# Attention of the first layers: half of the convolution and its norm behind the scores, two groups' squares summed on 32 columns each

## The chip, the cores and the metric

The kernel runs on one core of a Trainium2 chip. A core has a matrix engine (TensorE, PE in the profile, its weight loads as PEld), VectorE (DVE), ScalarE (ACT), GpSimd (POOL) and SyncE (SP), each with a queue of its own that it works through in order. The metric is the device time of one execution in microseconds (us).

## The reference

Four transformer layers on a sequence of 256 tokens and a width of 1024 in fp32. Layers 0 and 1 have a mixer with four parts of 256 features each; each part is brought to unit root mean square over its 256 features, multiplied by a gain, and the four go through the output projection:

```
outs = jnp.stack([short_conv_mixer(a_h, a_b, a_c, conv_w),   # group 0
                  nsa_mixer(...), gla_mixer(...), gmlp_mixer(...)], axis=2)   # groups 1, 2, 3
outs = rms_norm(outs, grp_gain.reshape(4, 256))
return outs.reshape(B, S, D_MODEL) @ w_o

def short_conv_mixer(h_in, b_gate, c_gate, conv_w):
    z = c_gate * h_in
    return b_gate * causal_conv_of_width_3(z, conv_w)
```

`nsa_mixer` is attention with three branches (compressed blocks, selected blocks, window), four heads of 64, summed with three gates. Layers 2 and 3 are of another kind and are not touched.

## The kernel before, in words

Features lie on partitions where this text speaks of columns: `oT` is 128 x 8 x 256, two chunks of 256 tokens for each group; `convT` holds the three inputs of the convolution in the same form. All matrix products with weights take three products of high and low halves; ScalarE makes the high half of a weight slot (L449), VectorE the low half (L458), GpSimd both halves of the activations (L890, L892). `rows_half` (L908) multiplies half a slot of the output projection into four banks of the accumulator PS. Everything is ordered by hand: each phase appends to the queue of each engine, and semaphores (`sig(...)`) join them. There is no barrier between phases.

In the phase `proj` (`gemm_phase`, L592) of layers 0 and 1 the short mixers run beside the input projection. VectorE's last piece of work there is the whole convolution (L1396 to L1406): one product of 128x512, then for each of two chunks one scaling (L1401) and two multiply-adds (L1404), and the gate product of 128x512 (L1406).

The phase `mixed` (`nsa_out_phase`) follows on each engine:

- TensorE: eight rounds of scores (L1562) in banks 3 to 7 and the compressed scores (L1613); the first four rounds come before, the last four after the sums of squares of groups 2, 3 and 0 (L1590, twelve products with one moving column, each recorded as two instructions); then `spread_group` for groups 2 and 3 (L1596), which writes a row of 1/rms over all partitions; transposes of the probabilities (L1571) and of the compressed ones (L1576), the first slot of the output projection (L908), the spread for group 0, the compressed branch (L1649), half of slot 1, then `attend(0, 0)` and `attend(1, 2)` (L1582, branches one and two of attention, 12 products each), the transposes of the finished heads (L436), and the rest of the output projection (L908, then L957), between which lie the sum and the spread for group 1.
- VectorE: masks and row maxima of the scores (L1730, L1737), the compressed scores (L1759 to L1764), the reciprocal of six columns of roots (L1766), the other scores with `normed(0)` and `normed(1)` among them (L1744), copies out of PS (L1787, L1790), `normed(2)` for the convolution's group, in layer 0 the modulation sums (L469, eight instructions), the weights of the branches (L1808), and the three branches: br 0 is L1817, br 1 and br 2 are L1819 and L1820 each. Then the copy of the heads to `oT` (L1827).
- ScalarE: three squares (L1671), the root (L1690), the exponentials (L1679), copies (L1683), weight halves (L449).

The order of VectorE between the copies and the branches, before the change:

```
normed(2, 2, 0)
for what, n, q, kk in todo:        # modulation sums, layer 0 only
    if what == "mod":
        mod_sums(dve, order, n, q, kk)
```

and of TensorE around the two `attend`s: `attend(0, 0)`, `pe.wait_ge(*on.at(6))`, `attend(1, 2)`. The signal `on` counts the halves of `normed`, two each; `gsum`, `grt`, `grc` and `gsp` count sums, roots, reciprocals and spreads.

## Time and profile before

| | us |
|---|---|
| median of 3 runs | 1518.88 (1517.07 to 1520.52) |
| profiled execution, its own time | 1518.78 |
| span of that execution | 1517.1 |
| TensorE busy | 1437.3 (95%) |
| VectorE busy | 1084.3 (71%) |
| ScalarE busy | 762.5 (50%) |
| mean granted TensorE clock | 0.988 of full |

The span is the time from the first to the last instruction; the time of the execution is 1.7 us longer. An engine's busy time counts its own instructions; a chain of waits is followed back from the last instruction of the program. PEclk is the granted TensorE clock: 1.00 is 2.4 GHz and 0.50 is 1.2 GHz.

### The profile page before, as it was taken

To read this page: it belongs to the slowest core of one execution; us is meant where nothing else is said; L and a number is where in the kernel's file an instruction comes from. 1 tells how busy PE (TensorE), PEld (TensorE's weight loads), DVE (VectorE), ACT (ScalarE), POOL (GpSimd) and SP (SyncE) were. 2 spreads that over 40 slices of the span, in tenths; PEclk is the share of its full clock that TensorE was granted. 3 is DMA by queue.
4 is the path that set the end of the run, shared out by engine and by line. 5 is a ranking of instruction groups with operands and counts; after the bars stand their busy time and mean duration, and the time that the engine had idled before them with its cause. 6 is when DMAs were issued, how large, how long until landed. Compare 5 with 4: busy or idle time off the path is not lost.

```text
span 1517.1 us, 24648 instructions
## 1 busy us (share of the span) xinstructions
PE 1437.3 (95%) x10229; PEld 1329.3 (88%) x10229; DVE 1084.3 (71%) x1448; ACT 762.5 (50%) x1097; POOL 406.7 (27%) x391
## 2 busy tenths in 40 slices
PE   2899899999999999999998899999999999999998
PEld 2888799977899799977998888999889998799987
DVE  5887797799557697799776567776477667565544
ACT  3556465534656465434875346444364444454432
POOL 0221320398121030397000321101419421220022
PEclk9999899999999999999999999999999999999999
DMA  9783659799352469798342025777557656455650
GB/s 392 278 321 118 236 232 350 290 350 346 112 209 84 165 267 347 286 350 330 139 168 98 1 87 215 287 288 261 194 191 283 218 218 226 172 198 219 223 207 28
DMA packets 49502, 340.71 MB, mean 225 GB/s; under 512 B 6640, under 2 KB 7024, under 8 KB 9072
## 3 DMA queue, kind: packets, MB, share of 16 engines
q1 hardware_dynamic: 46224, 333.04, 58.8%
q10 hardware_dynamic: 3168, 6.10, 1.1%
q8 instruction: 81, 1.33, 0.3%
q14 instruction: 29, 0.24, 0.0%
HBM read 338.04 MB, written 1.08 MB: 224 GB/s over the span
## 4 chain that ended last, share of the span: by engine, by line
PE 74%; DVE 10%; POOL 9%; issue 3%; ACT 3%; DMA 1%; SPq 0%; POOLq 0%; DVEq 0%; ACTq 0%
PE PS L592 48%; PE PS L908 14%; POOL acts_hi_lo L890 5%; POOL acts_hi_lo L892 4%; DVE ring L469 2%; DVE weights_hi_lo L458 1%; DVE X L1033 1%; PE PS L957 1%; PE PS L564 1%; DVE spare L771 1%; DVE arena L1030 1%; PE PS L2508 1%; DVE arena L1032 1%; ACT spare L736 1%; DMA X<-in_x_dram 1%
## 5 line engine op out<-in xcount | busy, mean ns | idle before, releaser
L458 DVE TENSOR_TENSOR weights_hi_lo<-ring,weights_hi_lo 128x1024 fp32r<-128x1024 f32 x426 | 550.5, 1316 | 279.1 <-ACT weights_hi_lo L449 278.0
L449 ACT ACTIVATE weights_hi_lo<-ring 128x1024 fp32r<-128x1024 f32 x426 | 444.7, 1058 | 476.4 <-PE PS L592 272.0
L592 PE MATMUL PS<-hi,weights_hi_lo 128*128 128x256 f32 x3456 | 546.2, 282 | 9.9 <-ACT hi L730 8.3
L592 PEld LDWEIGHTS PS<-hi,weights_hi_lo 128*128 128x128 f32 x3456 | 467.7, 189 | 13.0 <-issue 11.1
L908 PE MATMUL PS<-weights_hi_lo,acts_hi_lo 128*128 128x512 f32 x1584 | 377.6, 399 | 3.6 <-DVE heads L1730 2.0
L908 PEld LDWEIGHTS PS<-weights_hi_lo,acts_hi_lo 128*128 128x128 f32 x1584 | 298.4, 189 | 77.1 <-issue 2.7
L890 POOL CAST acts_hi_lo<-arena 128x256 fp32r<-128x256 f32 x142 | 134.3, 946 | 783.4 <-PE PS L908 436.0
L592 PE MATMUL PS<-lo,weights_hi_lo 128*128 128x256 f32 x1728 | 339.3, 281 | 0.0
L592 PEld LDWEIGHTS PS<-lo,weights_hi_lo 128*128 128x128 f32 x1728 | 263.0, 189 | 0.2 <-DVE lo L777 0.2
L469 DVE CUSTOM_DVE_ANT_0 ring<-ring,cond 128x1024 f32<-128x1024 f32 x192 | 253.2, 1356 | 9.7 <-DMA ring<-in_stream_dram 8.7
L892 POOL TENSOR_TENSOR acts_hi_lo<-arena,acts_hi_lo 128x256 fp32r<-128x256 f32 x142 | 170.1, 1198 | 11.4
L592 PE MATMUL PS<-weights_hi_lo,hi 128*128 128x256 f32 x928 | 150.8, 284 | 3.7 <-DVE weights_hi_lo L458 3.5
L592 PEld LDWEIGHTS PS<-weights_hi_lo,hi 128*128 128x128 f32 x928 | 127.4, 188 | 5.7 <-issue 5.5
L592 PE MATMUL PS<-weights_hi_lo,lo 128*128 128x256 f32 x464 | 93.2, 282 | 0.0
L592 PEld LDWEIGHTS PS<-weights_hi_lo,lo 128*128 128x128 f32 x464 | 71.7, 189 | 0.0
L712 PE MATMUL PS<-turning,X 128*128 128x128 f32 x256 | 33.9, 288 | 38.3 <-DVE turning L765 38.3
L712 PEld LDWEIGHTS PS<-turning,X 128*128 128x128 f32 x256 | 31.1, 199 | 40.6 <-DVE turning L765 40.6
L957 PE MATMUL PS<-weights_hi_lo,acts_hi_lo 128*128 128x512 f32 x192 | 46.3, 396 | 1.9 <-POOL acts_hi_lo L892 1.9
L2359 POOL TENSOR_TENSOR arena<-arena,constS 128x1024 f32<-128x1024 f32 x6 | 12.4, 2069 | 125.9 <-DVE arena L2276 119.6
L957 PEld LDWEIGHTS PS<-weights_hi_lo,acts_hi_lo 128*128 128x128 f32 x192 | 35.8, 187 | 11.4 <-POOL acts_hi_lo L892 2.8
L736 ACT ACTIVATE spare<-PS,mods 128x128 f32<-128x128 f32 x68 | 26.1, 454 | 9.2 <-DVE stat L875 5.1
L720 ACT ACTIVATE arena<-X 128x512 f32<-128x512 f32 x32 | 20.0, 625 | 19.7 <-DVE X L1033 11.6
(369 smaller groups left out, 1130.7 us busy)
## 6 DMA issues: line engine op xcount, KB each, us to landing
ring<-in_stream_dram SPq DMA_DIRECT2D x313, 1024.0 KB, 4.9
gate_row<-gate_rows_dram ACTq DMA_DIRECT2D x8, 512.0 KB, 3.6
constS<-in_const_dram SPq DMA_DIRECT2D x1, 1856.0 KB, 8.9
cond<-in_rows_dram SPq DMA_DIRECT2D x2, 512.0 KB, 5.2
X<-in_x_dram ACTq DMA_DIRECT2D x1, 1024.0 KB, 9.9
smallS<-in_small_dram SPq DMA_DIRECT2D x1, 883.0 KB, 8.0
out_dram<-X SPq DMA_DIRECT2D x2, 256.0 KB, 2.0
out_dram<-X ACTq DMA_DIRECT2D x2, 256.0 KB, 2.0
```

What stands on the lines that cost most here:

```text
L449: act.activation(wsp[:, g % 2, 0, at:at + HALF], ring[:, n % RING, at:at + HALF], ACT.Copy).then_inc(*ready.one())
L458: dve.tensor_tensor(wsp[:, g % 2, 1, at:at + HALF], ring[:, n % RING, at:at + HALF], wsp[:, g % 2, 0, at:at + HALF].bitcast(F32), ALU.subt ...
L469: ins = dve.tensor_tensor_reduce(w[:, r, :], w[:, r, :], cond[:, 0 if q < 12 else 1, :], 1.0, 0.0, ALU.mult, ALU.add, mods[:, q, k:k + 1])
L564: mm = pe.matmul(PS[:, 0, m * 256:(m + 1) * 256], h[:, k, m * P:(m + 1) * P], w[:, k, :], start=m + k + j == 0, stop=k == KD - 1 and j == ...
L592: mm = pe.matmul(o, lhs, rhs, start=k + g + j == 0, stop=k == KD - 1 and j == 2, skip_group_check=True)
L712: mm = pe.matmul(turned(2 * m + k // 4, k % 4), X[:, m, k * P:(k + 1) * P], turning[:, m, :], start=True, stop=True)
L720: act.activation(junk[:, u % 2, :], quarter(X, u), ACT.Square, accum_out=sums[:, u:u + 1]).then_inc(*xsq.one())
L736: ins = act.activation(buf(u)[:, k, :], turned(u, k), ACT.Identity, bias=mods[:, q, kk:kk + 1], scale=mods[:, q + 1, kk:kk + 1])
L890: pool.tensor_copy(asp[:, a % 2, 0, g, :], src).then_inc(*acts_hi.one())
L892: pool.tensor_tensor(asp[:, a % 2, 1, g, :], src, asp[:, a % 2, 0, g, :].bitcast(F32), ALU.subtract).then_inc(*acts_lo.one())
L908: mm = pe.matmul(PS[:, banks[2 * m + half], :], x[:, g, m * P:(m + 1) * P], w[:, g, half * WIDE:(half + 1) * WIDE], start=fresh and g + j ...
L957: mm = pe.matmul(PS[:, y_banks[u], :], x[:, g, m * P:(m + 1) * P], w[:, g, side * WIDE:(side + 1) * WIDE], start=fresh and last + g + j == ...
```

## The change

`convolve` is now a function for one chunk. In `proj` VectorE does the first product and chunk 0 only. In `mixed`, at the place where `normed(2)` stood, it does chunk 1 and the gate product; the sums for group 0 are taken alone, on bank 1, after half of slot 1; the reciprocal for it follows br 0, its spread stands between the two `attend`s, and `normed(2)` follows br 1. `attend(1, 2)` stands behind the wait for that reciprocal. The sums for groups 2 and 3 are taken by four products with 256 moving columns against 32 columns of ones, group 2 into partitions 0 to 31, group 3 into 32 to 63; the root and the reciprocal then work on 64x256 values, and two products of 64 rows against a column of the identity spread them.

```
...
             def token_major(i):
                 return 0 if i < 2 or i in CONV else (140 if i == 11 else 256)
             CONV = {8: 0, 9: 4, 10: 2}
+
+            def convolve(dve, order, ch):
+
+                z, y = convT[:, 4:6, :], oT[:, 0:2, :]
+                cw = prm(f"conv{l}")
+                if ch == 0:
+                    order(dve.tensor_tensor(z, z, convT[:, 0:2, :], ALU.mult))
+                tap = [cw[:, 3 * ch + j:3 * ch + j + 1] for j in range(3)]
+                order(dve.tensor_scalar(y[:, ch, :], z[:, ch, :], tap[2], None, ALU.mult))
+                for j in (1, 0):
+                    dl = 2 - j
+                    order(dve.scalar_tensor_tensor(y[:, ch, dl:], z[:, ch, :SEQ - dl], tap[j], y[:, ch, dl:],
+                                                   ALU.mult, ALU.add))
+
+            def gate_convolved(dve):
+                y = oT[:, 0:2, :]
+                return dve.tensor_tensor(y, y, convT[:, 2:4, :], ALU.mult)
+
             def proj(blk):
                 nsa_pe, nsa_act, blocks, rotation = nsa_inputs(l, kvcT, QK, VN)
-                pe, act, dve, pool = short_mixers(l, convT, lqT, lkT, lrT, LV, LG, MU, MV, oT, blocks, rotation)
+                pe, act, dve, pool = short_mixers(l, convT, lqT, lkT, lrT, LV, LG, MU, MV, oT, blocks, rotation, convolve)
                 gemm_phase(blk, ("proj", l), token_major, evac, banks=3, split_weights=True,
                            beside=(side_by_side(pe, nsa_pe), side_by_side(act, nsa_act), dve, pool))
 
-            return proj, lambda blk: nsa_out_phase(blk, l, VN, oT), oT[:, 2:4, :]
+            return proj, lambda blk: nsa_out_phase(blk, l, VN, oT, convolve, gate_convolved), oT[:, 2:4, :]
 
         def side_by_side(*works):
 
...
 
             return pe_beside, act_beside, blocks, rotation
 
-        def short_mixers(l, convT, lqT, lkT, lrT, LV, LG, MU, MV, oT, blocks, rotation):
+        def short_mixers(l, convT, lqT, lkT, lrT, LV, LG, MU, MV, oT, blocks, rotation, convolve):
 
 
 
...
             on = area(S + 2560, TT, 256)
             gsq, g = area(5920, 8, HD), area(6432, TT, 256)
             gw = prm(f"ws{l}").rearrange("p (g t) -> p g t", g=4)
-            cw = prm(f"conv{l}")
             dq = 32 ** -0.5
             taken = sig("gemm_bank_taken")
             zp, zb, ez, lz, dd, ee, kk, tr, tk = (sig(n) for n in (
...
             d4 = d.rearrange("p (n t) -> p n t", n=4)
             V8 = MV.rearrange("p m (h d) -> p (m h) d", d=HD)
             done = sig("short_mixed")
-            state["shorts_mixed"] = {"banks": done.at(2), 2: done.at(2), 3: done.at(1), 0: done.at(3)}
+            state["shorts_mixed"] = {"banks": done.at(2), 2: done.at(2), 3: done.at(1)}
 
             def pool_beside(pool):
                 order = Order(pool, "pool_order")
...
                 yield
 
                 dve.wait_ge(*taken.at(11))
-                z, y = convT[:, 4:6, :], oT[:, 0:2, :]
-                order(dve.tensor_tensor(z, z, convT[:, 0:2, :], ALU.mult))
-                for ch in range(2):
-                    tap = [cw[:, 3 * ch + j:3 * ch + j + 1] for j in range(3)]
-                    order(dve.tensor_scalar(y[:, ch, :], z[:, ch, :], tap[2], None, ALU.mult))
-                    for j in (1, 0):
-                        dl = 2 - j
-                        order(dve.scalar_tensor_tensor(y[:, ch, dl:], z[:, ch, :SEQ - dl], tap[j], y[:, ch, dl:],
-                                                       ALU.mult, ALU.add))
-                dve.tensor_tensor(y, y, convT[:, 2:4, :], ALU.mult).then_inc(*done.one())
+                convolve(dve, order, 0)
 
             def act_beside(act):
                 for _ in range(3):
...
 
             return pe_beside, act_beside, dve_beside, pool_beside
 
-        def nsa_out_phase(blk, l, VN, oT):
+        def nsa_out_phase(blk, l, VN, oT, convolve, gate_convolved):
 
 
 
...
                    heads[:, 3072:3584].rearrange("p (a k) -> p a k", a=4), heads[:, 3584:4096].rearrange("p (a k) -> p a k", a=4)]
             pcT, O, tmp = area(3872, 8, P), area(4896, TT, 256), area(5408, TT, 256)
             sq, gr = area(TEMP_AT, 4, 2, SEQ), stat[:, 64:72]
+            wide = 2
+            gw = sq[0:32 * wide, 3, 0, :]
             groups = (2, 3, 0, 1)
             scale = HD ** -0.5
             ready, taken = state.pop("nsa"), state.pop("taken")
             mixed = state.pop("shorts_mixed")
+            convolved = sig("convolved")
+            mixed[0] = convolved.at(1)
             cs, sd, ex, pc, pct, pcs, oc = (sig(n) for n in (
                 "cmp_scores", "cmp_shifted", "cmp_exp", "cmp_probs", "cmp_probs_T", "cmp_probs_T_taken", "cmp_out"))
             ws, wt, mxd, pe_, ptp, pta, ptd, ob = (sig(n) for n in (
...
                             mm = pe.matmul(PS[:, bank, col + m:col + m + 1], sq[:, i, c, m * P:(m + 1) * P], ones[:, 0:1],
                                            start=first and c + m == 0, stop=c == 1, skip_group_check=True)
                     return mm
+
+                def sums_at_once(bank):
+
+                    for c in range(2):
+                        for i in range(wide):
+                            if c == 0:
+                                pe.wait_ge(*gsq.at(i + 1))
+                            mm = pe.matmul(PS[32 * i:32 * i + 32, bank, 0:SEQ], ones[:, 0:32], sq[:, i, c, :], start=c == 0, stop=c == 1,
+                                           tile_position=(0, 32 * i), skip_group_check=True)
+                    return mm
+
+                def spread_row(i, bank, at, first):
+
+                    pe.matmul(PS[:, bank, at:at + SEQ], ident[0:32 * wide, 32 * i:32 * i + 1].to_broadcast((32 * wide, P)), gw,
+                              start=first, stop=True, skip_group_check=True).then_inc(*gsp.one())
 
                 def spread_group(i, bank, at, first):
                     for m in range(TT):
...
                             mm = pe.matmul(PS[:, bank, 16 * a:16 * a + CMP_N], qT[64 * e:64 * e + 64, k2, m * P:(m + 1) * P],
                                            kcT[64 * e:64 * e + 64, 0:CMP_N], start=True, stop=True)
                 mm.then_inc(*cs.one())
-                for i in range(3):
-                    mm = sums(i, 2, 2 * i, i == 0)
-                mm.then_inc(*gsum.one())
+                sums_at_once(2).then_inc(*gsum.one())
                 for r in range(4, 8):
                     scores(r)
                 pe.wait_ge(*grc.at(1))
-                spread_group(0, 2, 0, True)
-                spread_group(1, 2, 256, False)
+                spread_row(0, 2, 0, True)
+                spread_row(1, 2, 256, False)
                 turn_probs(1)
                 pe.wait_ge(*sd.at(1))
                 turn_probs(2)
...
                 turned_taken(pe, 2)
                 pe.wait_ge(*pc.at(1))
                 turn_cmp(0, 0)
-                pe.wait_ge(*on.at(4))
-                spread_group(2, 2, 0, True)
                 turned_taken(pe, 0)
                 turn_cmp(1, 3)
                 pe.wait_ge(*pcs.at(1))
...
                                        start=True, stop=True)
                 mm.then_inc(*oc.one())
                 rows_half(pe, slots[1], 0, y_banks, fresh=False)
+                sums(2, 1, 0, True).then_inc(*gsum.one())
                 turned_taken(pe, 3)
                 pe.wait_ge(*ready["gate"])
                 attend(0, 0)
-                pe.wait_ge(*on.at(6))
+                pe.wait_ge(*grc.at(2))
+                spread_group(2, 1, 0, True)
+                pe.wait_ge(*on.at(4))
                 attend(1, 2)
                 pe.wait_ge(*fin.at(1))
...
                 sums(3, 0, 0, True).then_inc(*gsum.one())
                 rows_half(pe, slots[2], 0, y_banks, fresh=False)
-                pe.wait_ge(*grc.at(2))
+                pe.wait_ge(*grc.at(3))
                 spread_group(3, 2, 0, True)
                 rows_half(pe, slots[2], 1, y_banks, fresh=False)
 
...
                     act.activation(pTs[q], PS[:, bank_of[q], :].rearrange("p (a k) -> p a k", a=4), ACT.Copy).then_inc(*pta.one())
 
                 stored = store_gate(act, l, 0, slots[0])
-                for i in range(3):
+                for i in range(2):
                     act.wait_ge(*mixed[groups[i]])
                     squares(i)
                 act.wait_ge(*gsum.at(1))
-                act.activation(gr[:, 0:6], PS[:, 2, 0:6], ACT.Sqrt, bias=cst("eps"), scale=1.0 / 256).then_inc(*grt.one())
+                act.activation(gw, PS[0:64, 2, 0:SEQ], ACT.Sqrt, bias=cst("eps")[0:64], scale=1.0 / 256).then_inc(*grt.one())
                 exponentials(0, 1)
                 exponentials(0, 0)
                 take_probs(1)
...
                     take_probs(q)
                 load_gate(act, l, 0, stored)
                 split_hi(act, slots[2])
+                act.wait_ge(*mixed[0])
+                squares(2)
+                act.wait_ge(*gsum.at(2))
+                act.activation(gr[:, 4:6], PS[:, 1, 0:2], ACT.Sqrt, bias=cst("eps"), scale=1.0 / 256).then_inc(*grt.one())
                 act.wait_ge(*nt.at(1))
                 squares(3)
                 for n in following:
                     split_hi(act, n)
-                act.wait_ge(*gsum.at(2))
+                act.wait_ge(*gsum.at(3))
                 act.activation(gr[:, 6:8], PS[:, 0, 0:2], ACT.Sqrt, bias=cst("eps"), scale=1.0 / 256).then_inc(*grt.one())
                 act.wait_ge(acts_lo.sem, 2 * last)
                 for g in range(2):
...
                 order(dve.tensor_reduce(mxc, scv, AX.X, ALU.max))
                 dve.tensor_tensor(scv, scv, bc(mxc, CMP_N), ALU.subtract).then_inc(*sd.one())
                 dve.wait_ge(*grt.at(1))
-                dve.reciprocal(gr[:, 0:6], gr[:, 0:6]).then_inc(*grc.one())
+                dve.reciprocal(gw, gw).then_inc(*grc.one())
                 scores_masked(4)
                 scores_masked(5)
                 row_max(1, 1)
...
                     dve.wait_ge(*pct.at(j + 1))
                     dve.tensor_copy(pcT[0:CMP_N, 4 * j:4 * j + 4, :],
                                     PS[0:CMP_N, bank, :].rearrange("p (a k) -> p a k", a=4)).then_inc(*pcs.one())
-                normed(2, 2, 0)
+                convolve(dve, order, 1)
+                gate_convolved(dve).then_inc(*convolved.one())
                 for what, n, q, kk in todo:
                     if what == "mod":
                         mod_sums(dve, order, n, q, kk)
...
                     dve.wait_ge(*done)
                     if br == 0:
                         order(dve.tensor_tensor(O8, src, bc(wgt[:, 0, :], HD), ALU.mult))
+                        dve.wait_ge(*grt.at(2))
+                        dve.reciprocal(gr[:, 4:6], gr[:, 4:6]).then_inc(*grc.one())
                     else:
                         order(dve.tensor_tensor(t8, src, bc(wgt[:, br, :], HD), ALU.mult))
...
                         if br == 1:
                             order(ins)
+                            normed(2, 1, 0)
                         else:
                             ins.then_inc(*fin.one())
                 split_lo(dve, slots[2])
...
                 dve.tensor_copy(oT[:, 2:4, :], PS[:, 3, :].rearrange("p (k t) -> p k t", k=2)).then_inc(*nt.one())
                 for n in following:
                     split_lo(dve, n)
-                dve.wait_ge(*grt.at(2))
+                dve.wait_ge(*grt.at(3))
                 dve.reciprocal(gr[:, 6:8], gr[:, 6:8]).then_inc(*grc.one())
                 normed(3, 2, 0)
```

## Rows read from the trace of the kernel before

**Rows 1.** The page: busy time of the engines, and the chain that ended last by engine.

```profile
PE 1437.3 (95%) x10229; PEld 1329.3 (88%) x10229; DVE 1084.3 (71%) x1448; ACT 762.5 (50%) x1097; POOL 406.7 (27%) x391
...
PE 74%; DVE 10%; POOL 9%; issue 3%; ACT 3%; DMA 1%; SPq 0%; POOLq 0%; DVEq 0%; ACTq 0%
```

**Rows 2.** Chain of work, layer 0: start us, us, what.

```profile
132.69 4.32 PE PS L1590 x24
...
143.35 5.82 PE PS L908 x24
...
159.37 1.14 DVE ring L469
```

**Rows 3.** Timeline of VectorE, layer 0: start, us, engine, line, operation [idle before, releaser].

```profile
130.12 0.35 DVE L1401 TENSOR_SCALAR arena<-arena,smallS 128x256 f32<-128x256 f32 x1
...
132.16 1.28 DVE L1730 SCALAR_TENSOR_TENSOR heads<-PS,constS 128x512 f32<-128x512 f32 x2
...
137.35 0.19 DVE L1766 RECIPROCAL stat<-stat 128x6 f32<-128x6 f32 x1 [0.26 <-ACT stat L1690]
139.05 1.29 DVE L1730 SCALAR_TENSOR_TENSOR heads<-PS,constS 128x512 f32<-128x512 f32 x2 [1.51 <-PE PS L1562]
...
141.51 0.86 DVE L1744 SCALAR_TENSOR_TENSOR arena<-arena,smallS,PS 128x256 f32<-128x256 f32 x2
...
149.64 0.69 DVE L1787 COPY constS<-PS 128x512 f32<-128x512 f32 x1 [0.52 <-PE PS L1571]
...
151.65 0.85 DVE L1744 SCALAR_TENSOR_TENSOR arena<-arena,smallS,PS 128x256 f32<-128x256 f32 x2
...
165.47 0.68 DVE L1817 TENSOR_TENSOR arena<-PS,later 128x512 f32<-128x512 f32 x1
...
167.63 0.69 DVE L1819 TENSOR_TENSOR arena<-PS,later 128x512 f32<-128x512 f32 x1
```

**Rows 4.** Timeline of TensorE, layer 0.

```profile
129.88 1.65 PE L1562 MATMUL PS<-constS 64*128 64x256 f32 x16 [0.59 <-ACT arena L1105]
...
149.88 0.61 PE L1596 MATMUL PS<-constS,stat 128*128 128x128 f32 x4
...
157.94 3.68 PE L1582 MATMUL PS<-arena,constS 128*128 128x64 f32 x32
...
169.11 1.11 PE L436 MATMUL PS<-constS,arena 128*128 128x128 f32 x4 [5.70 <-DVE arena L1820]
169.87 5.19 PE L908 MATMUL PS<-weights_hi_lo,acts_hi_lo 128*128 128x512 f32 x12
```

**Rows 5.** Stretches: busy us (x) of PE, PEld, DVE, ACT, POOL; granted PEclk, DMA.

```profile
134.00:140.00 6.00, 6.00 (x32) 5.43 (x31) 4.10 (x11) 3.13 (x8) 0.00 (x0) 0.50 0.00 0
...
164.50:174.00 9.50, 4.89 (x14) 4.03 (x15) 7.72 (x10) 1.57 (x2) 0.00 (x0) 0.50 0.71 271
...
499.00:502.00 3.00, 3.00 (x8) 2.35 (x8) 1.43 (x2) 0.14 (x1) 0.00 (x0) 0.50 0.38 102
```

**Rows 6.** VectorE's reciprocals grouped by shape, whole kernel: count | busy, mean ns | idle.

```profile
L764 DVE RECIPROCAL stat<-stat 128x1 f32<-128x1 f32 x16 | 2.5, 156 | 0.0
...
L1798 DVE RECIPROCAL later<-later 128x16 f32<-128x16 f32 x2 | 0.5, 242 | 0.0
...
L426 DVE RECIPROCAL stat<-stat 128x32 f32<-128x32 f32 x1 | 0.4, 354 | 1.9 <-ACT stat L431 1.9
```

**Rows 7.** Timeline of ScalarE, layer 0: the root of the six sums.

```profile
137.05 0.27 ACT L1690 ACTIVATE stat<-PS,constS 128x6 f32<-128x6 f32 x1 [2.84 <-PE PS L1590]
```

**Rows 8.** Chain of work, layer 1.

```profile
498.75 4.53 PE PS L908 x12
503.27 5.32 PE PS L1582 x48
...
514.74 2.90 PE PS L908 x12
```

**Rows 9.** VectorE's waits, 475 to 511 us: us in total, times, longest.

```profile
DVE arena L1819 <- PE PS L1582: 6.8, 2, 5.6
```

88 lines of the change are left out of this document (57 added, 31 removed).

## The prediction

> **What bounds the kernel now.** I read the page first. TensorE is busy 95% of the span and holds 74% of the chain that ended last [rows 1], so whatever the mixed phase of layers 0 and 1 gains or loses ahead of the output projection moves all that follows. Inside the phase it is not so simple, so I then read the chain, the timelines of the engines and the granted clock, layer by layer.
>
> Layer 0 has three parts. The first runs from the convolution to slot 0 of the output projection (L908, 143.35 us [rows 2]). Here VectorE is nearly always busy; it stands still only 0.26 us for the root and 1.51 us for the second half of the scores [rows 3]. These were late because the sums of squares hold TensorE for 4.32 us [rows 2] and the clock is at 0.50 from 134 to 140 us [rows 5]. In the second part, from the copy at 149.64 us to the last branch, VectorE is the bound: it goes without a pause through copies, modulation sums (eight of 1.14 us, of which one is shown [rows 2]) and branches [rows 3], while TensorE, done with both `attend`s, stands idle for 5.70 us [rows 4]. The third part is TensorE's again: transposes, then L908, which takes 5.19 us for twelve products [rows 4] where layer 1 needs 2.90 [rows 8], as the clock is at 0.50 until past 174 us [rows 5].
>
> In layer 1 there are no modulation sums. VectorE waits there 6.8 us in two pieces for the `attend`s [rows 9], and the chain goes through L908 and both `attend`s on TensorE [rows 8].
>
> **The first part of the phase.** Chunk 1 and the gate product leave the place ahead of the scores: from 130.12 to 132.16 us, 2.04 us [rows 3]. Not all of it is gained, since the first scores start at 129.88 us [rows 4] and four of their sixteen records have to end, 1.65 x 4/16 = 0.4 us and a tail of about 0.2: VectorE can begin its masks at 130.55 us in place of 132.16, 1.6 us earlier. From there to its wait for the root it had 4.93 us of work (132.16 to 137.09, the 137.35 of the reciprocal less its idle 0.26 [rows 3]), which now ends at 135.5.
>
> The sums fall from 24 records (4.32 us) to 8. Each is as wide as the score records, sixteen of which, half of them 128 wide, take 1.65 us: about 1 us for all. They end near 133.6, and the root (0.27 us before [rows 7], some 0.4 with 256 columns) near 134.1. Nobody waits for the root or the scores any more, which is 1.77 us of stalls removed.
>
> In their place comes a wider reciprocal. The trace has reciprocals of 1, 16 and 32 columns at 156, 242 and 354 ns [rows 6]: (354 - 156)/31 = 6.4 ns a column, 7.0 between the last two. For 256 columns this gives 1.78 to 1.92 us, and I take 1.85. The lower bound is the 0.35 us of a scaling of 128x256 (L1401) [rows 3], if the cost per column were one of narrow tiles alone. It stands squarely in VectorE's queue: the other half of the scores and both norms are behind it. So the second half of the masks starts at 135.5 + 1.9 = 137.4 in place of 139.05 [rows 3], and from `normed(0)` (141.51) over GpSimd's halves to slot 0 of the projection (143.35) all move 1.65 us forward. (If the reciprocal is cheap this is 3.1.)
>
> The Trainium skill ("VectorE: DVE Perf Modes", section "First, the fixed hardware budget") says that the reciprocal is an iterative division that is repeated 8 times; at the 0.96 GHz that the same page gives, 256 columns are an estimated 2.13 us, and each layer's sum would be some 0.3 us longer. The rows slope a little less steeply (6.4 to 7.0 ns a column against 8.3).
>
> **TensorE's clock in this part.** The denser sums keep TensorE from the light work during which the clock fell. But it is then done with the scores near 135, or 136 at the low clock, waits for the reciprocal until 137.4, spreads and transposes for some 1.5 us, and waits again until slot 0 at 141.7: about 4.5 idle us out of 6.7 just ahead of the 24 products of slot 0. That slot takes 5.82 us today at full clock [rows 2]. Elsewhere in this trace an idle time of 5.70 us was followed by L908 at half clock [rows 4, 5]. The low stretch of layer 1 [rows 5] costs 4.53 - 2.90 = 1.6 us [rows 8]. Its bounds are 0 and 2.3 us (5.19 - 2.90). I take half of 1.6, 0.8 us, in each layer.
>
> The Trainium skill ("TensorE: Matmul & The Clock Gate", section "HAM oscillation — how this bites in real kernels") says that a kernel whose bursts of products are separated by waits begins its bursts throttled. It speaks against this change, whose new waits come right ahead of products; by it the whole 1.6 us is paid in both layers and the sum is 1.6 us longer.
>
> **The second part, layer 0.** At the place of `normed(2)` (0.78 us, 151.65 to the next instruction) VectorE does chunk 1 and the gate product, 2.04 us: 1.26 more. Then after br 0 comes a reciprocal of two columns, 0.2 us with its handover. Br 0 ended at 165.47 + 0.68 = 166.15 [rows 3]; it now ends at 166.15 - 1.65 + 1.26 = 165.76, the reciprocal at 165.96. The sums and the root for it are long there (half of slot 1 and squares end near 157).
>
> Here is the step that decides. `attend(1, 2)` ran ahead of need before: TensorE was done at 163.4 (169.11 less 5.70 [rows 4]) and VectorE took its result from 167.63 [rows 3], 4.2 us of slack. Now it waits for the reciprocal, so it can't start before the modulation sums and br 0 are through. Behind that wait on TensorE stand the spread, `attend(1, 2)`, and all the rest of the projection; for them VectorE's br 2 waits. At full clock: spread 0.5 us (0.61 less its tail [rows 4]), `attend` half of 5.32 = 2.7 [rows 8], handovers 0.2, so 3.4 us, against VectorE's own cover of br 1 and `normed(2)`, 1.45 + 0.78 = 2.2. Br 2 would start at 169.4, 1.75 us later than before. At low clock: four transposes took 169.87 - 169.11 = 0.76 us, 0.19 us a record [rows 4]; 24 records of `attend` are 4.6, the spread 0.9, handovers 0.2, together 5.7. Br 2 starts at 171.7, 4.05 us later. TensorE ends `attend(0, 0)` near 157.94 + 2.7 - 1.65 + 0.9 = 159.9 and is idle for six us, as long as today's 5.70, at whose end the clock was at 0.50 [rows 5]. So I take 4.05. From the last branch on all keeps its order and its low clock.
>
> **Layer 1.** The same 1.65 us are gained ahead of slot 0. VectorE's additions lie beside its waits of 6.8 us [rows 9] and cost nothing; that cover would have to shrink by more than two thirds. On TensorE, which bounds this part, the sums for group 0 are added (eight records, 4.32/24 each at mostly low clock, 1.4; at full clock 0.9) and the spread moves from beside VectorE's copies into the chain (0.45). I take 0.9 + 0.45 = 1.35. Net -1.65 + 1.35 = -0.3. Whether the low stretch of today at 499 to 502 us [rows 5] stays, moves or goes is open: up to -1.6 or +2.
>
> **Costs taken at nothing.** The wider root and the square are on ScalarE, which waits 2.84 us for the sums today [rows 7]. GpSimd's halves for slot 2 come later, near 168.5 in layer 0, but are needed only after half of slot 1. No DMA is added or moved.
>
> **The sum.** Layer 0: +4.05 + 0.8 = +4.85. Layer 1: -0.3 + 0.8 = +0.5. Together +5.35 us on the profiled execution's 1518.78 us (span 1517.1 and 1.7 around it), 1524.1; that execution is 0.1 us from the median of the runs, so the median moves to the same place.
>
> **The rivals.**
> - The clock holds or costs nothing new. Br 2 of layer 0 is 1.75 us late, layer 1 is 0.3 us earlier: +1.45, 1520.3 us. For it: the clock stayed full through both `attend`s [rows 8]. Against it: the six idle us ahead of the second.
> - Faster, by the clock: the work moved behind the reciprocal has TensorE running from 166 us on in place of 169.1, so the clock is back when the transposes start. Twelve products of L908 then take 2.9 in place of 4.84 to 5.19 us, the transposes 0.4 less, and in layer 1 the low stretch goes: 1.45 - 2.3 - 0.4 - 1.6 = -2.85, 1515.9 us. With the cheap reciprocal another 1.5 us a layer, 1512.9. It decides once the clock reads 1.00 at the transposes of layer 0. Against it: narrow products of 64 columns did not keep the clock up when idle time came [rows 4, 5].
> - The low clock meets every burst: slot 0 fully (+1.5 more over both layers) and layer 1's half of slot 1 and `attend`s (+2): 1527.6 us.
>
> **How the numbers follow.** Likeliest case 0.48, clock-neutral 0.24, faster by the clock 0.13, low clock everywhere 0.15. The range goes from 1517.5, which leaves out most of the faster case, to 1529. A measurement of this kernel can tell 0.2%, 3.0 us, from no change. Slower by more: all of the low-clock case, most of the likeliest, 0.64; within: the neutral case and the edges of its neighbours, 0.25; faster by more: the part of the third case with the cheap reciprocal or more clock, 0.11.
>
> **What would show it.** In the profile after: a reciprocal of 64x256 of 1.8 us; masks starting near 130.6 and again near 137.4; no sums of over 1.2 us before the scores; an idle time of some six us on TensorE in layer 0 that ends with the reciprocal of two columns, the clock at 0.50 behind it, and VectorE waiting 1.3 to 3.5 us for L1582's successor before br 2. The forecast is wrong if `attend(1, 2)` of layer 0 starts well before 165 us, if the reciprocal takes a third of a microsecond, or if the clock is full in both output projections.

## The result and the profile after

The changed kernel takes 1533.41 us (median of 6 runs, 1529.82 to 1534.94) against 1519.70 before: a ratio of 1.0087 (1.0070 to 1.0104), slower by 13.2 us with an interval of 10.6 to 15.8. (1519.70 is the median of six runs; the 1518.88 given ahead of the prediction is that of the first three.) The direction was as forecast, and so was the wait that decides; the size was not: 5.35 us were forecast, and the time lies above the range's 1529.

The page of the profiled execution (span 1528.1 us, its own time 1529.82), engines and chain by engine:

```profile
PE 1443.0 (94%) x10205; PEld 1331.2 (87%) x10205; DVE 1086.0 (71%) x1450; ACT 764.8 (50%) x1099; POOL 393.1 (26%) x391
...
PE 72%; DVE 17%; POOL 5%; ACT 3%; issue 2%; DMA 1%; SPq 0%; POOLq 0%; DVEq 0%; ACTq 0%
```

Busy times hardly differ from [rows 1]; DVE's part of the chain has grown from 10 to 17%. VectorE in layer 0 after the change, to be laid beside [rows 3] (this execution reaches the mixed phase 2.91 us later: ScalarE's last copy of the projection, L1105, starts at 132.24 in place of 129.33):

```profile
134.00 1.29 DVE L1760 SCALAR_TENSOR_TENSOR heads<-PS,constS 128x512 f32<-128x512 f32 x2 [1.01 <-PE PS L1574]
...
138.86 1.74 DVE L1796 RECIPROCAL arena<-arena 64x256 f32<-64x256 f32 x1
140.52 1.22 DVE L1760 SCALAR_TENSOR_TENSOR heads<-PS,constS 128x512 f32<-128x512 f32 x2
...
152.54 0.69 DVE L1817 COPY constS<-PS 128x512 f32<-128x512 f32 x1 [1.89 <-PE PS L1583]
...
169.57 0.17 DVE L1850 RECIPROCAL stat<-stat 128x2 f32<-128x2 f32 x1
...
171.12 0.87 DVE L1774 SCALAR_TENSOR_TENSOR arena<-arena,smallS,PS 128x256 f32<-128x256 f32 x2
176.06 0.69 DVE L1852 TENSOR_TENSOR arena<-PS,later 128x512 f32<-128x512 f32 x1 [4.07 <-PE PS L1594]
```

The stalls before the second masks are gone, and the wide reciprocal stands there. The new stall is the last row: VectorE waits 4.07 us for `attend` before br 2. TensorE of the same execution, beside [rows 4]:

```profile
135.53 1.06 PE L1612 MATMUL PS<-arena,constS 128*32 128x256 f32 x8
...
140.65 1.55 PE L1618 MATMUL PS<-arena,constS 64*128 64x256 f32 x4 [2.45 <-DVE arena L1796]
...
144.75 7.32 PE L908 MATMUL PS<-weights_hi_lo,acts_hi_lo 128*128 128x512 f32 x24 [0.65 <-DVE heads L1760]
...
169.79 1.23 PE L1623 MATMUL PS<-constS,stat 128*128 128x128 f32 x4 [3.72 <-DVE stat L1850]
170.80 1.81 PE L1594 MATMUL PS<-arena,constS 128*128 128x64 f32 x8
172.40 3.62 PE L1594 MATMUL PS<-arena,heads 128*128 128x64 f32 x16
...
178.30 4.79 PE L908 MATMUL PS<-weights_hi_lo,acts_hi_lo 128*128 128x512 f32 x12
```

Slot 0 takes 7.32 us in place of 5.82 [rows 2], and everything from the spread (L1623) to the first half of the projection behind the transposes is slow. Two stretches of this execution, columns as in [rows 5], say why; the clock column is the third from the end:

```profile
141.50:147.50 6.00, 5.35 (x17) 3.77 (x16) 5.25 (x13) 4.52 (x19) 3.03 (x6) 0.50 0.00 0
169.00:180.00 11.00, 8.70 (x36) 8.23 (x37) 6.75 (x11) 0.00 (x0) 2.19 (x4) 0.50 0.39 163
```

For all that follows I measure a mixed phase from the start of ScalarE's copy L1105 to the first record of the last projection products (L957), which TensorE reaches in the same order in every kernel here. Slot 0 is the duration of its 24 records.

| kernel (profiled execution) | its time | phase, layer 0 (slot 0) | phase, layer 1 (slot 0) |
|---|---|---|---|
| before | 1518.78 | 52.51 (5.82) | 47.52 (5.82) |
| before again (x12) | 1518.85 | 52.57 (5.82) | 48.28 (5.83) |
| changed | 1529.82 | 57.63 (7.32) | 50.11 (6.86) |
| changed again (x1) | 1527.07 | 56.87 (6.83) | 49.91 (7.87) |
| changed (x13) | 1533.11 | 56.04 (5.82) | 54.94 (7.96) |
| changed (x14) | 1526.31 | 56.21 (5.82) | 50.21 (6.97) |
| changed (x15) | 1536.85 | 57.40 (7.18) | 54.92 (7.95) |

The means of the five executions of the changed kernel, less those of the two of before, are +4.3 us in layer 0 and +4.1 in layer 1, 8.4 together. What lies outside the phases took 1418.0 and 1418.8 us in the two executions of before and 1419.9 to 1424.5 in the five of the changed kernel.

### The profile page after: what moved, and what is told of

The parts are those of the page before. It is cut to its first block, busy times and chain, and to the rows that moved or that the text cites. A ratio compares the mean times of both kernels' runs of the same rounds, so it can differ in the third digit from the quotient of the medians.

```text
span 1528.1 us, 24606 instructions
## 1 busy us (share of the span) xinstructions
PE 1443.0 (94%) x10205; PEld 1331.2 (87%) x10205; DVE 1086.0 (71%) x1450; ACT 764.8 (50%) x1099; POOL 393.1 (26%) x391
## 4 chain that ended last, share of the span: by engine, by line
PE 72%; DVE 17%; POOL 5%; ACT 3%; issue 2%; DMA 1%; SPq 0%; POOLq 0%; DVEq 0%; ACTq 0%
PE PS L592 47%; PE PS L908 14%; DVE weights_hi_lo L458 5%; DVE ring L469 4%; POOL acts_hi_lo L890 2%; POOL acts_hi_lo L892 2%; DVE X L1033 1%; PE PS L957 1%; ACT weights_hi_lo L449 1%; PE PS L564 1%; DVE spare L771 1%; DVE arena L1030 1%; PE PS L2542 1%; PE PS L1594 1%; DVE arena L1032 1%
## 5 line engine op out<-in xcount | busy, mean ns | idle before, releaser
L592 PE MATMUL PS<-hi,weights_hi_lo 128*128 128x256 f32 x3456 | 546.0, 282 | 9.8 <-ACT hi L730 8.3
L592 PEld LDWEIGHTS PS<-hi,weights_hi_lo 128*128 128x128 f32 x3456 | 467.5, 189 | 12.9 <-issue 11.1
L908 PE MATMUL PS<-weights_hi_lo,acts_hi_lo 128*128 128x512 f32 x1584 | 382.6, 402 | 2.3 <-DVE weights_hi_lo L458 1.4
L908 PEld LDWEIGHTS PS<-weights_hi_lo,acts_hi_lo 128*128 128x128 f32 x1584 | 302.2, 192 | 77.4 <-issue 2.7
L592 PE MATMUL PS<-lo,weights_hi_lo 128*128 128x256 f32 x1728 | 338.5, 280 | 0.0
L890 POOL CAST acts_hi_lo<-arena 128x256 fp32r<-128x256 f32 x142 | 122.0, 859 | 802.5 <-PE PS L908 437.3
L592 PEld LDWEIGHTS PS<-lo,weights_hi_lo 128*128 128x128 f32 x1728 | 262.2, 188 | 0.0
L592 PE MATMUL PS<-weights_hi_lo,hi 128*128 128x256 f32 x928 | 152.8, 287 | 5.2 <-DVE weights_hi_lo L458 5.0
L592 PEld LDWEIGHTS PS<-weights_hi_lo,hi 128*128 128x128 f32 x928 | 129.3, 191 | 7.3 <-issue 7.1
L592 PE MATMUL PS<-weights_hi_lo,lo 128*128 128x256 f32 x464 | 94.1, 284 | 0.0
L592 PEld LDWEIGHTS PS<-weights_hi_lo,lo 128*128 128x128 f32 x464 | 72.5, 191 | 0.0
L957 PE MATMUL PS<-weights_hi_lo,acts_hi_lo 128*128 128x512 f32 x192 | 46.3, 396 | 2.0 <-DVE weights_hi_lo L458 1.1
L957 PEld LDWEIGHTS PS<-weights_hi_lo,acts_hi_lo 128*128 128x128 f32 x192 | 35.8, 187 | 11.5 <-issue 1.5
```

What stands on the lines that cost most here:

```text
L592: mm = pe.matmul(o, lhs, rhs, start=k + g + j == 0, stop=k == KD - 1 and j == 2, skip_group_check=True)
L890: pool.tensor_copy(asp[:, a % 2, 0, g, :], src).then_inc(*acts_hi.one())
L908: mm = pe.matmul(PS[:, banks[2 * m + half], :], x[:, g, m * P:(m + 1) * P], w[:, g, half * WIDE:(half + 1) * WIDE], start=fresh and g + j ...
L957: mm = pe.matmul(PS[:, y_banks[u], :], x[:, g, m * P:(m + 1) * P], w[:, g, side * WIDE:(side + 1) * WIDE], start=fresh and last + g + j == ...
```

## The experiments

Times are medians; every ratio is to the kernel before, run beside it. A difference to the changed kernel carries the interval of that kernel too (1.0060 to 1.0117 beside x1), some 4 us either way.

| run | us | ratio (95%) | mean granted clock |
|---|---|---|---|
| x1 changed kernel again | 1533.40 | 1.0089 (1.0060 to 1.0117) | 0.9843 |
| x2 attend first | 1525.54 | 1.0040 (1.0026 to 1.0053) | 0.9900 |
| x3 narrow sums | 1525.67 | 1.0030 (1.0014 to 1.0046) | 0.9873 |
| x4 sums only | 1524.60 | 1.0030 (1.0016 to 1.0044) | 0.9880 |
| x5 both undone | 1522.65 | 1.0016 (1.0004 to 1.0027) | 0.9892 |
| x6 changed, waits filled | 1523.75 | 1.0019 (1.0007 to 1.0031) | 0.9938 |
| x7 before, filled | 1519.22 | 0.9989 (0.9975 to 1.0003) | 0.9908 |
| x8 x5, filled | 1524.36 | 1.0024 (1.0004 to 1.0045) | 0.9906 |
| x9 filled ahead of slot 0 | 1527.62 | 1.0045 (1.0030 to 1.0060) | 0.9879 |
| x10 filled ahead of attend | 1524.16 | 1.0034 (1.0017 to 1.0050) | 0.9903 |
| x11 layer 1 only | 1517.93 | 0.9987 (0.9976 to 0.9999) | 0.9912 |
| x12 before again | 1518.60 | 0.9990 (0.9977 to 1.0004) | 0.9885 |

The clock column is the mean over the timed runs. For the kernel before it was 0.9876 to 0.9883 in these three sets, some 36 us at 1.2 GHz in 1520 (twice the missing share, since only the two levels occur); for the first six runs of the changed kernel it was 0.9822, 55 us. At 1.2 GHz a product takes at most twice its time here (3.62 us for 16 records of `attend` against 1.95), so these 19 us more at the low clock can have cost some 9 us at most, an estimate.

**x1: the changed kernel again.** No edit.

> The changed kernel once more, for a second profile. Theory A: the 13.7 us are the steps in the mixed phases alone; then the first projection of layer 0 (L592 behind 84 us) runs at full clock this time, the 2.9 us that the first profile lost there do not come back, and the mixed phases still lose 7 to 10 us together. Theory B: the change itself costs clock outside the mixed phases; then the same 2.9 us are lost again in front of 130 us. Both expect a ratio of 1.007 to 1.010 to the kernel before.

The ratio repeats. This time the copy L1105 starts at 129.09 us, so the 2.9 us lost ahead of the mixed phase in the first profile were not the change's: theory A. Over all profiles that copy starts anywhere between 128.8 and 132.4 us, in x4, x7 and x12 too, whose code up to there is that of before (132.44, 131.46 and 129.96). But the two phases are only 6.8 us longer here, just under the 7 to 10 expected and well under the 13.2.

**x2: attend(1, 2) ahead of the wait.**

```
                 attend(0, 0)
-                pe.wait_ge(*grc.at(2))
-                spread_group(2, 1, 0, True)
                 pe.wait_ge(*on.at(4))
                 attend(1, 2)
+                pe.wait_ge(*grc.at(2))
+                spread_group(2, 1, 0, True)
```

> The changed kernel with attend(1, 2) ahead of the wait for the two-column reciprocal and of the spread, as the only edit. Theory A: the stall of VectorE ahead of br 2 in layer 0 (4.07 us) goes, TensorE has its long idle time back; layer 1 gains nothing or loses up to 1 us, since the spread now comes behind attend(1, 2). 4 to 5 us faster than the changed kernel, about 1527 to 1529 us. Rival (the clock alone): the low clock stays around the last branch and the projection, so under 2 us faster.

The gain over the changed kernel is 7.9 us by the medians (1533.40 to 1525.54) and 7.4 by the ratios, above the 4 to 5 expected but not by more than the interval. TensorE, layer 0:

```profile
162.82 1.95 PE L1594 MATMUL PS<-arena,heads 128*128 128x64 f32 x16
165.83 0.71 PE L1623 MATMUL PS<-constS,stat 128*128 128x128 f32 x4 [1.06 <-DVE stat L1850]
169.48 1.12 PE L436 MATMUL PS<-constS,arena 128*128 128x128 f32 x4 [2.93 <-DVE arena L1853]
```

`attend` runs at full clock (1.95 us for the records that took 3.62) well before it is needed, and the transposes wait for VectorE as they did in [rows 4]. The order on TensorE's queue is the cause of the stall; the rival (under 2 us) falls.

**x3: narrow sums for groups 2 and 3.**

```
-                sums_at_once(2).then_inc(*gsum.one())
+                for i in range(2):
+                    mm = sums(i, 2, 2 * i, i == 0)
+                mm.then_inc(*gsum.one())
```

with root and reciprocal on four columns and `spread_group` for both.

> The changed kernel with the sums of groups 2 and 3 as before (one moving column each, four columns of roots), so that only the convolution and the norm of group 0 are moved. Theory A: the reciprocal of 64x256 (1.74 us) goes from VectorE's queue, the sums take 2.9 us in place of 1.06; VectorE reaches slot 0 of the projection about 0.5 to 1 us earlier, and slot 0 meets no low clock since TensorE idles less ahead of it: 1 to 4 us faster than the changed kernel, 1529 to 1532 us. Rival (the wide sums are worth it): the narrow sums make the scores late again, 1 to 3 us slower than the changed kernel.

Faster than the changed kernel by 7.7 us, where 1 to 4 were expected; the rival had the sign wrong. VectorE's reciprocal, and TensorE's sums and slot 0 in layer 0 (two views):

```profile
137.76 0.17 DVE L1798 RECIPROCAL stat<-stat 128x4 f32<-128x4 f32 x1
```

```profile
134.44 1.95 PE L1602 MATMUL PS<-constS,arena 128*128 128x1 f32 x16
...
142.12 7.40 PE L908 MATMUL PS<-weights_hi_lo,acts_hi_lo 128*128 128x512 f32 x24 [1.55 <-DVE heads L1762]
```

Narrow sums of two groups cost 0.9 us more than the wide ones, and the narrow reciprocal 1.6 less, where it is on the path. Slot 0 starts 10.97 us into the phase in both layers (12.50 in the changed kernel, 14.02 and 13.79 before). These 1.5 us a layer are 3 of the 7.7; the profile doesn't tell what the rest is, and layer 0's phase, 56.21 us, is as long as in the changed kernel. Slot 0 met the low clock here in layer 0, and not in layer 1 (5.84), whose phase took 46.05 us, the shortest of all. The wide sums with their reciprocal are thus a loss by themselves in this order; that slot 0 is spared the low clock without it, as I had expected, is not shown by layer 0.

**x4: the sums only.** The kernel before, with three groups at once and the convolution left in front:

```
+            wide = 3
+            gw = sq[0:32 * wide, 3, 0, :]
...
-                for i in range(3):
-                    mm = sums(i, 2, 2 * i, i == 0)
-                mm.then_inc(*gsum.one())
+                sums_at_once(2).then_inc(*gsum.one())
```

> The kernel before with all three groups' sums taken at once on 32 columns each and the 96x256 root and reciprocal, the convolution left whole ahead of the scores. Theory A: no attend behind a reciprocal, so no stall in layer 0; VectorE pays 1.55 us for the wide reciprocal and gets back 1.77 (layer 0) and 1.06 us (layer 1) of waits; the low clock can meet slot 0. Between 1 us faster and 4 us slower than before, 1518.5 to 1523.5. Rival (the sums are the main loss, by the clock): 6 us or more slower than before.

4.4 us slower than before by the medians and 4.6 by the ratio, just past the edge of theory A's 4. TensorE's idle time ahead of the spread, and slot 0 behind it:

```profile
141.91 2.08 PE L1608 MATMUL PS<-arena,constS 96*128 96x256 f32 x4 [2.68 <-DVE arena L1781]
...
146.00 6.85 PE L908 MATMUL PS<-weights_hi_lo,acts_hi_lo 128*128 128x512 f32 x24 [0.31 <-DVE heads L1745]
```

So with the wide sums slot 0 can meet the low clock without any part of the move; in layer 1 it did not (5.84), and in the profiles with the sums of before in both layers (before, x7, x12) it never did (5.82 to 5.84). But this does not explain the 4.4 us: the phases of this profile take 51.82 and 48.52 us, together 100.3, as before (100.0 and 100.9), and the 7 us by which the execution is slower (1526.00) lie outside them, in code that is the same. Where x4 loses its time is open.

**x5: both undone.** x2, x3, and `normed(2)` behind br 2 in place of br 1. What is left is the moved half of the convolution, with the sums, the spread and the norm of its group as late as it makes them.

> The changed kernel with both narrow sums for groups 2 and 3 and attend(1, 2) ahead of the wait; the norm of group 0 goes behind br 2, so that in layer 1 VectorE does not wait there for the spread. What is left of the change is the moved half of the convolution. Theory A (two separate losses, the attend behind the reciprocal and the wide reciprocal with the idle TensorE ahead of slot 0): the two gains of 7.8 us found singly mostly add, 1516 to 1520 us, at or under the kernel before. Rival (both experiments only moved the same low clock about): no more than one of the gains, 1524 to 1526 us.

1522.65: more than one of the gains and less than their sum, and the forecast of 1516 to 1520 missed; by the ratio it is 2.4 us slower than before (0.6 to 4.1). The phases take 52.18 and 47.42 us in its profile, 0.3 and 0.1 less than before. So the moved half of the convolution has won nothing in this order. In layer 0 slot 0 starts 1.15 us earlier, and VectorE gives that back behind the copies, where the convolution takes 1.2 us more than the norm did. In layer 1 it starts 2.4 us earlier, but the norm behind br 2 makes the copy of the heads late, and TensorE waits 1.42 us for the squares of it. What the moved half would be worth with the norm elsewhere is not shown.

**x6: the waits filled.** This is the run that bears on the price of the clock. All of the changed kernel's order stays; TensorE multiplies an idle tile where it would wait.

```
                 for r in range(4, 8):
                     scores(r)
+                idle_products(pe, 18, 3)
                 pe.wait_ge(*grc.at(1))
...
                 turn_probs(2)
+                idle_products(pe, 16, 1)
...
                 attend(0, 0)
+                pe.wait_ge(*on.at(4))
+                if l == 0:
+                    idle_products(pe, 45, 2)
                 pe.wait_ge(*grc.at(2))
```

> The changed kernel with idle products on TensorE in its new waits: 18 ahead of the wait for the wide reciprocal and 16 ahead of slot 0 in both layers, 45 ahead of the wait for the two-column reciprocal in layer 0. Nothing else is changed. Theory A (the size that I missed is the low clock, met by slot 0, by the spread and attend(1, 2) and by the projection): slot 0 takes 5.8 us, the stall ahead of br 2 falls from 4.07 to 1.2 to 1.8 us, and the time falls by 6 to 10 us to about 1524 to 1527. Rival (the waits themselves cost, whatever the clock): under 3 us, or slower since idle products delay.

The ratio falls from 1.0089 to 1.0019, 10.6 us by the ratios and 9.7 by the medians, with 113 more products on TensorE (2 x 34 and 45) and not a dependency less. TensorE in layer 0 and the stretch around slot 0:

```profile
143.57 5.84 PE L908 MATMUL PS<-weights_hi_lo,acts_hi_lo 128*128 128x512 f32 x24 [0.21 <-issue]
...
163.21 5.22 PE L662 MATMUL PS<-idle 128*128 128x128 f32 x45
168.27 0.66 PE L1623 MATMUL PS<-constS,stat 128*128 128x128 f32 x4
168.76 1.00 PE L1594 MATMUL PS<-arena,constS 128*128 128x64 f32 x8
169.60 1.95 PE L1594 MATMUL PS<-arena,heads 128*128 128x64 f32 x16
```

```profile
137.00:154.00 17.00, 15.86 (x101) 12.86 (x100) 13.63 (x27) 12.41 (x42) 5.43 (x8) 1.00 0.00 1
```

VectorE's wait ahead of br 2:

```profile
171.59 0.69 DVE L1857 TENSOR_TENSOR arena<-PS,later 128x512 f32<-128x512 f32 x1 [1.68 <-PE PS L1594]
```

4.07 us have become 1.68, and slot 0 takes 5.84. The waits themselves are thus not what costs most: 10 of some 13 us go without one of them being removed. That is not the same as 10 us lost to the clock by the change. By the mean clocks the changed kernel spends 48 to 55 us at 1.2 GHz, the kernel before 36 and x6 only 19: the filling has also given back what the kernel before loses (its twelve products behind the transposes of layer 0 take 3.98 us here, 5.19 in [rows 4]). If the gain is shared out by these times, the change's own 12 to 19 us of low clock are worth some 4 to 5 us, an estimate, and 6 to 9 at the very most; the phases, below, give 5.8. Against the kernel before as it is, 0.0019 or 2.9 us (1.1 to 4.7) are left; against x7 below, the kernel before with one wait filled, 0.0030 or some 4.6. My clock-neutral rival had said 1.45.

**x9 and x10: one filling at a time.** The first two insertions of x6 alone, then the third alone.

> The changed kernel with idle products only ahead of slot 0 (18 before the wait for the wide reciprocal, 16 before slot 0, both layers); 45 products of x6 ahead of the second attend are left out. Theory A: slot 0 takes 5.8 us in both layers in place of 5.5 to 7.9; of the 9.7 us that x6 won it brings 3 to 4, about 1529.5 us. Rival (the clock at slot 0 is most of it): 6 us or more.

> The changed kernel with idle products only ahead of the wait for the two-column reciprocal in layer 0 (45). Theory A: the spread and attend(1, 2) of layer 0 run at full clock, 3.3 us in place of 6.2, and part of the projection behind them gains too: 4 to 6 us, about 1528.5 us; x9 and x10 together make the 9.7 us of x6. Rival: under 2 us, as the low clock then meets the projection instead.

x9 wins 0.0044 (6.7 us; 5.8 by the medians) and x10 0.0055 (8.4 us), both above theory A's 3 to 4 and 4 to 6, x9 about at its rival's "6 us or more"; together 0.0099, more than x6's 0.0070. With intervals of some 0.0015 on each and more on the changed kernel, I can say that both places matter and not how they share, and x9's rival is not excluded. In x10's profile slot 0 of layer 1 still takes 7.63 us; in x9's the spread and `attend` of layer 0 are still slow.

**x7 and x8: filling the kernel before, and x5.**

```
                 attend(1, 2)
+                if l == 0:
+                    idle_products(pe, 45, 1)      # x8: behind a wait for the root of group 0
```

> The kernel before with 45 idle products in the idle time of TensorE ahead of the transposes of layer 0 and no other edit. Theory A: the clock stays full, the transposes and twelve products take 3.5 us in place of 6: 2 to 3 us faster than before, about 1517.5. Rival: the clock falls later or the idle products delay the transposes: no change within 1 us.

> x5_both_undone with 45 idle products behind attend(1, 2) in layer 0, ahead of the wait for the two-column reciprocal. Theory A: another 2 to 3 us on top of x5, 1514 to 1517, faster than both kernels. Rival: the spread comes late behind the idle products and holds up the transposes, no gain over x5.

TensorE of x7, layer 0:

```profile
165.34 5.22 PE L662 MATMUL PS<-idle 128*128 128x128 f32 x45
171.24 0.66 PE L436 MATMUL PS<-constS,arena 128*128 128x128 f32 x4 [0.68 <-DVE arena L1822]
171.65 3.02 PE L908 MATMUL PS<-weights_hi_lo,acts_hi_lo 128*128 128x512 f32 x12
```

The transposes and twelve products are as fast as foreseen (1.11 and 5.19 us in [rows 4]) and the phase of layer 0 takes 50.35 us, 2.2 less. The timed gain, 0.0011, is not distinguishable from nothing. x8 is a miss of its own making, and its rival was right. TensorE, then VectorE:

```profile
166.02 5.22 PE L662 MATMUL PS<-idle 128*128 128x128 f32 x45
171.08 0.66 PE L1623 MATMUL PS<-constS,stat 128*128 128x128 f32 x4
...
176.79 1.05 PE L1602 MATMUL PS<-constS,arena 128*128 128x1 f32 x8 [1.82 <-ACT arena L1702]
```

```profile
171.78 0.87 DVE L1779 SCALAR_TENSOR_TENSOR arena<-arena,smallS,PS 128x256 f32<-128x256 f32 x2 [1.80 <-PE PS L1623]
```

The idle products ran on until the spread, VectorE waited for it in front of `normed(2)`, and the copy of the heads behind that came late for ScalarE's squares, for which TensorE then waited: the copy starts 44.28 us into the phase, 42.67 in x5.

**x11: the move where nothing stands behind it, and x12: before against itself.** Layer 0 is x7's, layer 1 x3's.

> Layer 0 as in the kernel before with 45 idle products ahead of its transposes (x7), layer 1 with the moved convolution and norm and narrow sums (x3), where the mixed phase took 46.05 us in x3's profile against 47.52 before. Theory A (the move costs only where modulation sums stand between it and the reciprocal): 3 to 4 us faster than before, a ratio of 0.9975 to 0.998. Rival (layer 1's 1.5 us in x3 were clock): no faster than x7, a ratio of 0.999.

> The kernel before against itself: a ratio of 1.000 within 0.001, and a second profile of it. If the low clock ahead of the mixed phases (2.9 us at 84 us in the first profile of the changed kernel) is nothing of the change, it can show here too.

x11 has the shortest phases of all kernels taken together, 48.69 and 46.62 us, and the lowest median, 1517.93. Its ratio of 0.9987 reaches up to 0.9999, but the kernel before against itself gives 0.9990. The 3 to 4 us expected are not shown, although the phases of its profile are 5 us shorter than before, and I claim no kernel faster than before.

**x13 to x15: where the rest lies.** The changed kernel, three single executions.

> The changed kernel, one execution and its profile. The first two profiled executions (1529.82 and 1527.07 us) were the fastest of their sets of six. If an execution near the median of 1533.4 us is caught, theory A expects its further 4 to 6 us as lower clock inside the two mixed phases (slot 0 up to 7.9 us, half of slot 1 and the second attend of either layer), the stretches between them at 291 to 293 us as before. Rival: the further time lies outside the mixed phases.

> As x13_draw: another execution of the changed kernel, with the same two expectations.

> As x13_draw: a third execution of the changed kernel, with the same two expectations.

x13 (1533.11 us) and x15 (1536.85) have what the first two profiles had missed: layer 1 takes 54.9 us. TensorE of x15 in layer 1, and the granted clock:

```profile
493.52 7.95 PE L908 MATMUL PS<-weights_hi_lo,acts_hi_lo 128*128 128x512 f32 x24 [1.88 <-DVE heads L1760]
...
512.60 2.93 PE L1594 MATMUL PS<-arena,constS 128*128 128x64 f32 x24
515.32 1.17 PE L1623 MATMUL PS<-constS,stat 128*128 128x128 f32 x4
...
517.88 3.62 PE L1594 MATMUL PS<-arena,heads 128*128 128x64 f32 x16
523.02 1.12 PE L436 MATMUL PS<-constS,arena 128*128 128x128 f32 x4 [1.51 <-DVE arena L1853]
523.78 5.37 PE L908 MATMUL PS<-weights_hi_lo,acts_hi_lo 128*128 128x512 f32 x12
```

```profile
513.00:515.30 2.30, 2.30 (x23) 2.30 (x22) 0.17 (x1) 0.04 (x1) 0.00 (x0) 0.99 0.02 7
515.30:523.00 7.70, 6.21 (x30) 6.02 (x29) 3.68 (x7) 0.00 (x0) 2.19 (x4) 0.50 0.00 0
...
516.00:528.00 12.00, 10.49 (x41) 9.43 (x40) 6.61 (x10) 1.58 (x2) 2.19 (x4) 0.50 0.16 43
```

Before any long idle time, in the run of narrow products that the change has lengthened (sums of one column, `attend`, spread, `attend`), the clock fell and stayed at 1.2 GHz until the projection had run for some us. In the other three executions layer 1 took 49.9 to 50.2 us. That the added sums and spread are what let the clock fall there is likely and not tested: no run takes them alone out of layer 1. Theory A's expectation holds: between the layers these executions need 291.4 to 292.4 us, against 291.4 before.

## Why the prediction was wrong

*The step that decides* was right: `attend(1, 2)` of layer 0 waits for a reciprocal that stands behind the modulation sums. The spread and `attend` were put at 5.7 us at low clock and took 6.26 (169.79 to 176.05); `attend` took 5.22 us (170.80 to 176.02), 0.22 a record, where I had the transposes' 0.19. TensorE's idle time ahead of it was 3.72 us and not six; 1.5 us of the difference are the half of slot 1 before it, which ran at the low clock in all five executions (4.4 to 4.6 us, 3.07 before) and cost nothing while VectorE was the bound. The clock was at 0.50 behind the shorter wait too. The phase of layer 0 grew by 5.1 us in the profiled execution and by 4.3 in the mean of five; 4.85 was forecast.

*The first part* was close. The masks start 1.76 us into the phase in place of 2.83: 1.07 us gained and not 1.6, because VectorE got its first scores 1.2 us after TensorE began them, where I had put 0.7. The reciprocal holds VectorE for 1.66 us in place of 1.85 (1.74 us long; 96 partitions take the same). Slot 0 starts 1.51 us earlier against 1.65 forecast. The repeat count of 8 of the Trainium skill ("VectorE: DVE Perf Modes", section "First, the fixed hardware budget") had given an estimate of 2.13 us, which is above the 1.74 measured.

*VectorE's additions in the second part* held: 2.02 us stand where `normed(2)` took 0.78.

*The term that was mis-sized is TensorE's clock*, "I take half of 1.6, 0.8 us, in each layer", together with layer 1's low stretch, "up to -1.6 or +2", which I had taken at nothing. At slot 0 of layer 0 the five executions lose 0.8 us in the mean, as put; at slot 0 of layer 1 they lose 1.7 (7.52 against 5.82). And in two of five, layer 1 lost another 5 us behind it, more than the bound of 2. Layer 1 was forecast at +0.5 and came out at +4.1. Its parts, means of five less means of two: slot 0 starts 1.2 us earlier (1.65 forecast); the sums, both `attend`s and the spread take 1.6 us more at full clock (1.35 forecast), which makes +0.4 without the clock; the rest is low clock, 1.7 us at slot 0, 1.1 in the narrow products (x13 and x15 alone) and 1.0 from the transposes on. So the clock took 3.7 us there, where 0.8 had been put. The section "HAM oscillation — how this bites in real kernels" of the page "TensorE: Matmul & The Clock Gate" of the Trainium skill speaks of such throttled bursts, and had the right sign. The case that I had worked out beside it from rows, 1.6 us more, would have made 6.95, still well short. The mistake behind the number was to price one low stretch at slot 0, and to let the low clock in layer 1's narrow products and projection, which may come or go, cancel out to nothing. In layer 0 the clock took 0.8 us at slot 0 and 1.8 in the spread and `attend` (from the sums to the transposes 15.15 us, 13.34 with the wait filled in x6 and x10), and 0.5 came back behind them. Together 5.8 of the phases' 8.4 us are clock and 2.6 order, where the sum had 3.9 and 1.45; what it had too little of is mostly layer 1's clock. x6 agrees in that the time comes back when the waits are filled, though it gives back more than the change had lost.

*The range* reached to 1529 through the low-clock rival of 1527.6. That rival named the right mechanism, but gave layer 1 no more than 2 us and its share of slot 0, where the two long executions show 7 (54.9 against 47.9).

*Not settled.* The phases account for 8.4 us of the 11.8 by which the five profiled executions are slower in the mean; the other 3.4 lie ahead of, between and behind the phases, in code that is the same. In four profiles whose code outside the phases is that of before, these parts took 1418.0, 1418.8, 1425.7 and 1426.0 us (before, x12, x4, x7), and 1421.8 in the mean of the five, so chance would do, and no run shows more. The timed runs of x4 and x5 are slower than before by 4.6 and 2.4 us while their profiled phases are not longer; that is open too. The runs don't tell either why the low clock comes in some executions and not in others of the same kernel.

## What to carry to other kernels

When work is moved behind a wait on one engine, count what stands behind that wait in its queue, and ask how long ahead of need it ran before: here 4.2 us of slack were spent. When the engine is TensorE, price each new wait and each longer run of narrow products at the low clock for what comes next as well, from both levels, and forecast the mean over executions and not the one that was profiled. A wide tile that saves products can cost more in the element-wise step behind it: 0.9 us saved in the sums, 1.6 us paid in the reciprocal.

## What the runs showed of the hardware

- The reciprocal costs about 6.2 ns a column also on a wide tile: 1.74 us at 256 columns for 64 partitions and for 96 (x4) alike, against 156 ns at one column [rows 6].
- Products on 32 columns of the array into different column groups did not overlap. The eight records of the changed kernel take 1.06 us, the twelve of x4 1.38 us, and the next product starts 0.99 and 1.31 us after the first of them: 0.11 to 0.12 us a record of 256 moving columns, about as for the full-width records of L592 (four in 0.48 us from start to start).
- The clock fell in x15 while TensorE was busy without a gap (2.30 of the 2.30 us before 515.30, at 0.99), in products of 64 moving columns, and stayed at 0.50 through some 6 us more of such narrow products.
- Filling waits raised the mean clock of the timed runs from 0.9843 to 0.9938 in the changed kernel. Where the filling ended before the wait did it delayed nothing: slot 0 starts 12.51 us into the phase of layer 0 with it (x6) and without it. Where it ran on past the reciprocal (x8) VectorE waited 1.80 us for the spread.
